# Attention times values: the values' high and low parts as one operand, four matmuls a group instead of six

## The reference

```python
qkv = u @ wqkv
q = rmsnorm(q, gq); k = rmsnorm(k, gk)             # 16 query heads, 4 key/value heads, head size 64
qb = q.reshape(b, nb, BLK, KV, G, HD)              # 8 blocks of 128 queries
kb, vb = band(k), band(v)                          # the block before and this one: 256 keys
scores = einsum('bnqkgd,bnskd->bnkgqs', qb, kb) * HD ** -0.5
scores = where(mask, scores - slopes * dist, -inf) # 128 keys are in the window of each query
m = maximum(scores.max(-1), sink)
e = exp(scores - m)
probs = e / (e.sum(-1) + exp(sink - m))
o = einsum('bnkgqs,bnskd->bnqkgd', probs, vb)      # <- the changed product
return o.reshape(b, s, H * HD) @ wo
```

## Time and profile before

| | us |
|---|---|
| median of 3 runs | 1079.7 (1078.48 to 1079.87) |
| profiled execution, its own time | 1078.62 |
| its span in the profile | 1076.9 |
| PE busy / PEld busy | 1059.7 (98%) / 876.6 (81%) |
| VectorE / ScalarE / GpSimd busy | 783.7 (73%) / 471.9 (44%) / 169.2 (16%) |
| granted PE clock | full in every slice |

### The profile page before, as it was taken

The page is one execution under the profiler, slowest core; times in us unless marked ns, Lnnn a source line. Parts: engine busy times, 40 slices in busy tenths (PEclk is TensorE's granted clock), DMA queues, the critical chain, the costliest instruction groups (busy, mean ns, idle before and its releaser), DMA issues.

```text
span 1076.9 us, 14194 instructions
## 1 busy us (share of the span) xinstructions
PE 1059.7 (98%) x4936; PEld 876.6 (81%) x4936; DVE 783.7 (73%) x1127; ACT 471.9 (44%) x819; POOL 169.2 (16%) x277
## 2 busy tenths in 40 slices
PE   7899999999999999999999999999999999999998
PEld 5778888887888888888888888888888888888887
DVE  6877777788344599776677668476776878747985
ACT  6566666677323233412322342353333334437451
POOL 8665555553000000000000000000000000001000
PEclk9999999999999999999999999999999999999999
DMA  8101110050332325353343244998998898760102
GB/s 313 46 34 40 40 40 21 37 196 20 118 117 79 117 71 205 135 195 117 144 188 140 92 188 187 372 412 286 285 290 291 290 321 302 254 234 1 40 30 88
DMA packets 67468, 171.74 MB, mean 159 GB/s; under 512 B 5200, under 2 KB 5456, under 8 KB 67280
## 3 DMA queue, kind: packets, MB, share of 16 engines
q1 hardware_dynamic: 67408, 170.95, 44.4%
HBM read 133.18 MB, written 37.75 MB: 159 GB/s over the span
## 4 chain that ended last, share of the span: by engine, by line
PE 88%; DVE 5%; POOL 3%; issue 2%; ACT 2%; ACTq 0%; POOLq 0%; DVEq 0%
PE pair L2530 28%; PE pair L2510 22%; PE pair L2256 9%; PE pair L2393 8%; PE pair L2576 7%; PE pair L2322 3%; PE pair L2468 3%; PE pair L2290 2%; PE pair L2605 2%; PE pair L2301 1%; PE pair L2438 1%; POOL bias L840 1%; ACT probs L1048 1%; PE pair L2275 1%; PE pair L2235 0%
## 5 line engine op out<-in xcount | busy, mean ns | idle before, releaser
L2530 PE MATMUL pair<-uT 128*128 128x512 f32 x1344 | 305.9, 389 | 0.0
L2530 PEld LDWEIGHTS pair<-uT 128*128 128x128 f32 x1344 | 252.0, 188 | 52.5 <-DVE uT L1959 0.4
L1304 ACT ACTIVATE uT<-wo_raw 128x1024 fp32r<-128x1024 f32 x83 | 84.8, 1054 | 114.1 <-PE pair L2530 97.2
L1959 DVE TENSOR_TENSOR uT<-wo_raw,uT 128x1024 fp32r<-128x1024 f32 x83 | 98.6, 1222 | 46.1 <-ACT uT L1304 45.6
L785 POOL TENSOR_SCALAR row_var<-row_ssq 128x1 f32<-128x1 f32 x16 | 4.0, 250 | 706.4 <-ACT hn L1345 623.2
L2393 PE MATMUL pair<-WA,oT 128*128 128x512 f32 x384 | 90.3, 392 | 0.5 <-DVE oT L1719 0.3
L2393 PEld LDWEIGHTS pair<-WA,oT 128*128 128x128 f32 x384 | 71.2, 188 | 15.8 <-issue 1.3
L2510 PE MATMUL pair<-WA,WB 128*128 128x512 f32 x336 | 78.2, 389 | 0.4 <-ACT xr L1279 0.4
L2510 PEld LDWEIGHTS pair<-WA,WB 128*128 128x128 f32 x336 | 63.0, 188 | 13.8 <-DVE WB L1893 0.8
L2576 PE MATMUL pair<-WA 128*128 128x512 f32 x288 | 68.1, 391 | 0.0
L2576 PEld LDWEIGHTS pair<-WA 128*128 128x128 f32 x288 | 53.7, 188 | 11.0
(11 more groups left out here) (242 smaller groups left out, 1884.9 us busy)
## 6 DMA issues: line engine op xcount, KB each, us to landing
wo_raw<-in_m_w SPq DMA_DIRECT2D x71, 512.0 KB, 6.7
wo_raw<-hid_kept SPq DMA_DIRECT2D x41, 512.0 KB, 6.2
hid_kept<-RES SPq DMA_DIRECT2D x32, 512.0 KB, 2.7
emb<-in_m_w SPq DMA_DIRECT2D x17, 512.0 KB, 6.2
RES<-in_m_w SPq DMA_DIRECT2D x8, 1024.0 KB, 6.7
uT_f<-in_m_w SPq DMA_DIRECT2D x6, 1024.0 KB, 6.9
RES<-in_a_wqkv SPq DMA_DIRECT2D x10, 512.0 KB, 8.3
emb<-hid_kept SPq DMA_DIRECT2D x10, 512.0 KB, 6.1
```

Of the source, the lines that this page charges most:

```text
L1304: nc.scalar.activation(operand(t, which, HI), unit(t, which), ACT.Copy).then_inc(op_hi, 1)
L1959: nc.vector.tensor_tensor(operand(t, which, LO), unit(t, which), operand(t, which, HI).bitcast(F32), ALU.subtract).then_inc(op_ready, 1)
L2530: mm = nc.tensor.matmul(ps[4 * (j % 2) + m][:], operand(t, 0, s)[:, k, m * P:(m + 1) * P], operand(t, 1, r)[:, k, :], start=(g == 0 and k ...
```

## The change

`vz` is laid out anew: for each key/value head its 64 high columns and its 64 low columns stand side by side. One stationary operand is now [high | low] of one head, and one matmul gives the high part's product in the upper 64 rows of the result and the low part's in the lower 64. A group takes 2 x 2 matmuls: that operand by the high and by the low part of `pT`, for `kt` 1 and 0 (so low by low is computed too). The two halves of the rows have to be added: ScalarE copies the lower half into `RES` (`low_out`, told by the new semaphore `lows_out`), VectorE adds the upper half from PSUM to it in place (`attention_out`, now VectorE's) and tells `attended`. `current_ready` goes, its steps are counted by `zeros_ready`.

```diff
-        vz = sb("vz", [P, 2, 2, KV * HD], F32R, in_a)
+        vz = sb("vz", [P, 2, KV, 2, HD], F32R, in_a)
@@ GpSimd
-                copy(vz[:, 0, HI, :], vprev[:]).then_inc(dv_moved, 1)
+                copy(vz[:, 0, :, HI, :], by_head(vprev)).then_inc(dv_moved, 1)
@@ ScalarE
-                nc.scalar.activation(vz[:, 1, HI, :], vnext[:], ACT.Copy).then_inc(v_hi, 1)
+                nc.scalar.activation(vz[:, 1, :, HI, :], by_head(vnext), ACT.Copy).then_inc(v_hi, 1)
-            def attention_out(n, j):
+            def low_out(n, j):
...
-                mine = slice(HD * (j % 2), HD * (j % 2 + 1))
                 flat = RES[:].rearrange("p b n -> p (b n)")
                 for odd in range(2):
                     moved = nc.scalar.activation(flat[odd * HD:(odd + 1) * HD, bass.ds(n * D + j * 2 * P, 2 * P)],
-                                                 pv_bank[mine, odd * 2 * P:(odd + 1) * 2 * P], ACT.Copy)
-                moved.then_inc(attended, 1)
+                                                 pv_bank[HD:P, odd * 2 * P:(odd + 1) * 2 * P], ACT.Copy)
+                moved.then_inc(lows_out, 1)
@@ VectorE
-                nc.vector.tensor_tensor(vz[:, 1, LO, :], vnext[:], vz[:, 1, HI, :].bitcast(F32),
+                nc.vector.tensor_tensor(vz[:, 1, :, LO, :], by_head(vnext), vz[:, 1, :, HI, :].bitcast(F32),
                                         ALU.subtract).then_inc(v_ready, 1)
...
+            def attention_out(n, j):
+
+                dve.wait_ge(lows_out, 4 * n + j + 1)
+                for odd in range(2):
+                    o = RES[:].rearrange("p b n -> p (b n)")[odd * HD:(odd + 1) * HD, bass.ds(n * D + j * 2 * P, 2 * P)]
+                    out = nc.vector.tensor_tensor(o, pv_bank[0:HD, odd * 2 * P:(odd + 1) * 2 * P], o, ALU.add)
+                out.then_inc(attended, 1)
...
                         pT_lo_part(t - 1, (j - 1) % 2)
+                    if not (first and j < 2):
+                        attention_out(*before(n, j, 2))
                     if j == 0:
                         v_diff(n)
                     if j == 1:
...
+            attention_out(NB - 1, GROUPS - 2)
             pT_lo_part(NB * GROUPS - 1, 1)
             oT_lo_half(1, 1)
+            attention_out(NB - 1, GROUPS - 1)
@@ TensorE
-                    for s, m in PASSES:
+                    for m in (HI, LO):
 
-                        at = 2 * HD * (j // 2)
-                        mm = nc.tensor.matmul(pv_bank[:], vz[:, kt, s, at:at + 2 * HD], pT[:, m, kt, :],
-                                              start=(done == 0), stop=(done == 5))
+                        mm = nc.tensor.matmul(pv_bank[:], vz[:, kt, j, :, :].rearrange("p s d -> p (s d)"), pT[:, m, kt, :],
+                                              start=(done == 0), stop=(done == 3))
```

More of the change, by code:

```diff
@@ L405, in trunk_layer @@
         dist_step = sem("dist_step")
-        current_ready = sem("current_ready")
+        lows_out = sem("lows_out")
         bias_first = sem("bias_first")
@@ L545, in trunk_layer, with by_head @@
         turn_bank = ps[6]
+        def by_head(v):
+            return v[:].rearrange("p (v d) -> p v d", d=HD)
         def q_rows(odd, s):
@@ L812, in _ @@
             pool.memset(vprev[:], 0.0).then_inc(zeros_ready, 1)
-            pool.memset(current[:], 1.0).then_inc(current_ready, 1)
-            pool.wait_ge(current_ready, 1)
+            pool.memset(current[:], 1.0).then_inc(zeros_ready, 1)
+            pool.wait_ge(zeros_ready, 3)
             pool.affine_select(out=current[:], in_=current[:], compare_op=ALU.is_ge, fill=0.0,
-                               base=0, pattern=[[-1, P]], channel_multiplier=1).then_inc(current_ready, 1)
+                               base=0, pattern=[[-1, P]], channel_multiplier=1).then_inc(zeros_ready, 1)
             pool.iota(dist[:], pattern=[[-1, 2 * P]], base=P, channel_multiplier=1,
@@ L1081, in last_part @@
                     pT_hi_part(t - 1, (j - 1) % 2)
-                    attention_out(n - 1, 2)
+                    low_out(n - 1, 2)
                     q_hi_part("q8", n, 0)
@@ L1090, in last_part @@
                 pT_hi_part(t - 1, (j - 1) % 2)
-                attention_out(*before(n, j, 2))
+                low_out(*before(n, j, 2))
                 if j == 1:
@@ L1187, in _ @@
             body(NB - 1, 1, last=True)
-            attention_out(NB - 1, GROUPS - 2)
+            low_out(NB - 1, GROUPS - 2)
             pT_hi_part(NB * GROUPS - 1, 1)
@@ L1191, in _ @@
             oT_hi_half(2, 0)
-            attention_out(NB - 1, GROUPS - 1)
+            low_out(NB - 1, GROUPS - 1)
             oT_hi_half(2, 1)
@@ L1581, in v_lo_part @@
                 dve.wait_ge(v_hi, b + 1)
-                nc.vector.tensor_tensor(vz[:, 1, LO, :], vnext[:], vz[:, 1, HI, :].bitcast(F32),
+                nc.vector.tensor_tensor(vz[:, 1, :, LO, :], by_head(vnext), vz[:, 1, :, HI, :].bitcast(F32),
                                         ALU.subtract).then_inc(v_ready, 1)
                 dve.wait_ge(dv_moved, 2 * b + 1)
-                nc.vector.tensor_tensor(vz[:, 0, LO, :], vprev[:], vz[:, 0, HI, :].bitcast(F32),
+                nc.vector.tensor_tensor(vz[:, 0, :, LO, :], by_head(vprev), vz[:, 0, :, HI, :].bitcast(F32),
                                         ALU.subtract).then_inc(v_ready, 1)
@@ L1591, in add_bias @@
                 if first:
-                    dve.wait_ge(current_ready, 2)
+                    dve.wait_ge(zeros_ready, 4)
                 for half_bank in range(2):
@@ L1633, in pT_lo_part, with before @@
                                         ALU.subtract).then_inc(pT_ready, 1)
+            def attention_out(n, j):
[4 more added lines that the diff above has]
+                out.then_inc(attended, 1)
+            def before(n, j, lag):
+                return (n, j - lag) if j >= lag else (n - 1, j - lag + GROUPS)
             def last_part(n, j):
```

## The result

The changed kernel takes 1085.9 us (median of 4 runs, 1085.1 to 1086.8), the kernel before 1079.1 us beside it (4 runs, 1078.5 to 1079.9): ratio 1.0063, 95% interval 1.0045 to 1.008. It is 6.8 us slower, outside my range; I had forecast no change. The profiled execution took 1085.6 us.

What follows compares the result with a forecast made beforehand. VectorE's loop, with one group's PE matmuls in it, bounds the kernel. Blocks 1 to 5 -1.9, registers +0.4, blocks 6 and 7 +0.8: -0.7 us, so 1079.0 us; own bounds 1077 to 1081, 8 in 10 1075.2 to 1084.0.

Steps and rivals of the forecast that it cites:

- kn without its wait: Each block: the added pair before kn takes 0.70 us, covered by kn's 0.68 us wait for GpSimd's k_rstd.
- the 98%: PE's busy share of the span on the profile page; matmul busy time was said to flatter PE, weight loads showing 81%.
- The pair: VectorE's two added 64x256 adds per group, taken at 0.70 us, bounds 0.68 and 1.7; 32 pairs 22 us.
- the wait for the mask: After a block's first pair, v's first low part waits until 165.00 for GpSimd's mask of pT's low part.
- The allowance of 0.4 us for register instructions: Blocks 2 to 5: register instructions on the adds, 0.1 us a pair, counting at the second pair: +0.4 us.
- The third rival: Pairs hold VectorE longer, counting at 16 places; at 1.1 us a pair 1085.4 us; chance 0.22.
- The step that failed most: Blocks 1 to 5: pairs delaying the score additions of groups 0 and 1 add nothing to the loop.
- Block 7: Four added pairs, 2.8 us, 1.3 remaining after absorption; PE saves 0.46: +0.8 us, block 6's gain included.
- what I let be absorbed: Block 7: 0.4 us from block 6, about 0.4 collision, up to 0.5 idle before 243.39, 0.2 smaller gaps.
- A whole group's work of 7 us lies before the next use: PE's wait for the PSUM bank (attended), now released by VectorE's adds, was forecast to cost nothing.
- The first rival: Block 7 keeps PE's gain, 4 x 0.46 us, pairs falling in VectorE's idle time: -3.8 us, 1075.9 us; chance 0.20.
- the collision: Blocks 1 to 5: v's second low part stood behind GpSimd's mask; avoiding this gains 0.38 us a block, -1.9 us.

Runs made afterwards that it cites:

- the run with one joined group: Changed kernel with the [high | low] operand and VectorE's adds only for group 2 of blocks 0 to 5, six matmuls elsewhere (64-column operands): 1078.1 us.
- the warm start: 14 identity transposes on PE before block 0's first scores, added to the kernel with group 2 of blocks 0 to 5 joined and the scaling moved: 1074.35 us.
- the adds alone: Kernel before, keeping its six matmuls a group, plus VectorE's pair of adds behind ScalarE's copies: 1089.9 us, ratio 1.0093.

## Why the prediction was wrong

- **The bound** was right: a loop on VectorE, in which only one group's matmuls of PE count. The groups of four matmuls, the distance before the scores (1.53 to 1.68 us, about 2 forecast), kn without its wait and v's low parts of 0.42 us came as written, and the run without adds shows 0.46 us a block. That the 98% flatter PE was my word: the Trainium skill (Perfetto Trace Analysis, Identifying the Most-Contended Engine) says that matmul busy time is not a good measure, and not that it flatters.
- **The pair was under-sized**: 0.70 us taken, 0.87 measured. I had scaled rows at full partitions on one operand kind; the row of pT's low part, one PSUM and one SBUF input, 512 columns in 0.69 us, gives for two instructions of 256 columns more than 0.70 if any fixed part is counted twice, and 0.70 left none. With the scaling moved, the cost of this in blocks 1 to 5 can be read against the kernel before. At the first pair the excess itself vanishes in the wait for the mask, as in my reckoning: v's first low part starts 1.48 us after pT's, 1.50 forecast. But from pT's low part to the copy on the scores it is 2.15 us, 1.94 before and 2.03 forecast, since the two low parts take 0.34 us each from start to start, where I had 0.28 and 0.25. From the next pT's low part to kn it is 1.47 to 1.50 us instead of 1.36: the pair shows by 0.13 us behind the wait that was to cover it. And from kn to kT's low part, where I had added nothing, it is 0.29 us more in blocks 2 and 3 and 0.05 us more in 4 and 5, not traced. Over five blocks that is 1.1 + 0.7 + 0.7 = 2.4 us of VectorE against 2.3 us less of PE's part: +0.1 us, where I had -1.5. The allowance of 0.4 us for register instructions was not needed: outside the loop with registers the pairs take the same 0.83 to 0.85 us. The third rival had the direction (slower from 0.88 us a pair), and at 0.87 its own sum gives only +2.7 us over mine: it is not what decided.
- **The step that failed most** is "VectorE waits later in both groups for ScalarE and GpSimd, and the loop's start, PE at 158.60, does not depend on them". I dismissed the two pairs ahead of the score additions of groups 0 and 1 for lying beside idle time. The second of them, that of the block before's group 2, is enough, as the run with one joined group shows: nmax of group 1 goes from 0.7 us ahead of GpSimd's scaling to 0.34 us behind its start, and then it is in the loop, since the exponentials wait for it: 2.6 us in blocks 1 to 5, shown by moving the scaling. I had checked the adds against the mask, and not whether the instructions they delay meet something new.
- **Block 7**: +0.8 us forecast for blocks 6 and 7, +3.1 measured. Four pairs at 0.87 instead of 0.70 are 0.7 us, the fallen clock 0.7 us. The rest, 0.9 us, I leave open. The unforeseen wait for the adds of group 25 (1.01 us) is one candidate, not tested by itself. Another is what I let be absorbed: up to 0.5 us in VectorE's idle time of 0.50 us before pT's low part (243.39), which is still there after the change:

```profile
248.07 0.69 DVE L1635 TENSOR_TENSOR pT<-pair,pT 128x512 fp32r<-128x512 f32 x1 [0.60 <-ACT pT L1061]
```

"A whole group's work of 7 us lies before the next use" holds in blocks 1 to 6, where PE never waits for the adds, and failed in block 7, where the first group's turn took 3.87 us before the change (237.40 to 241.27).
- **The first rival** (block 7 keeps PE's gain) fell with that. **The start**: 1.2 us, of which 0.3 lies before the first scores in either profile and the rest goes with the clock's fall; the warm start shows that the fall is PE's idleness there, not the change's. In the run with the scaling moved, whose clock didn't fall there, block 0 takes 28.8 us with all its pairs, as before.
- **The range** was too narrow by its own terms: with the collision kept (+1.9) and block 7 at its upper bound (+1.5) together, the forecast reaches 1082.4 us and not 1081. The measured 1085.9 lies above even that, because the stall of nmax and the clock were in no term.

## What to carry to other kernels

When work is added to an engine beside idle time, list the instructions it delays and ask what each now runs beside on the other engines; a small instruction can stand behind a long one for all of its length. A change that moves work from a saturated engine to its neighbour pays only at the places where the first engine's work lies in the loop and the neighbour's in slack: here the kernels with 6 or 12 joined groups of 32 and the scaling moved gain 4.3 to 5.1 us (some 1.5 of it by the form of their other groups), all 32 lose 6.8. Price a split operation per instruction, from a row with the same kinds of operands. And when a run turns a change off in part, check that the part turned off is the old kernel's; here it was not quite.

## What the runs showed of the hardware

- An add of 64x256 with one PSUM and one SBUF input, in place, takes 0.42 us, a pair of them 0.83 to 0.85 us in the changed kernel, with the next instruction 0.86 to 0.88 us after the pair's start; one of 64x512 takes 0.68 us, with the next 0.60 us after its start.
- nmax (128x4, two SBUF inputs, 0.16 us) took 0.91 to 1.88 us when it started during GpSimd's scaling of 128x1024 (1.90 us) and more than 0.25 us before its end: 1.56 to 1.88 us for group 1 in six kernels with the scaling at its old place, 0.91 to 1.22 us for group 0 in three with it moved. Each time it ended 0.01 to 0.03 us after the scaling, which was no longer than otherwise.
- The granted clock fell to 0.50 behind idle stretches of PE of 2.1 to 2.6 us: in block 0 behind 2.34 us in 45 of 63 executions of the kernel before (by their mean clock), in block 7 behind 2.62 us in both profiles that have it, behind 2.41 us with the single add and behind 2.09 us with the adds alone. It stayed there for 3 to 4 us, once for 6.8 us. Transposes of an identity in the idle time (14 and 12) prevented it, worth about 0.7 us each.
- ScalarE's copies of 64x256 from PSUM start 0.60 to 0.63 us after the start of the 128x512 copy ahead of them when they read rows 64 to 127 of the bank, and 0.47 to 0.50 us after it when they read rows 0 to 63, in all runs and in all groups but the last two, whose copies wait for their matmuls.
